# Six of the eleven down blocks of each FFN: half of each computed by seven products of 2x2 block sums

## What is computed

```python
def _swiglu(h, w_gu, w_down):
    g, u = jnp.split(h @ w_gu, 2, axis=-1)
    return (jax.nn.silu(g) * u) @ w_down

x = x + 0.5 * _rmsnorm(_swiglu(_rmsnorm(x, ffn1_pre_g), ffn1_w_gu, ffn1_w_down), ffn1_post_g)
...
x = x + 0.5 * _rmsnorm(_swiglu(_rmsnorm(x, ffn2_pre_g), ffn2_w_gu, ffn2_w_down), ffn2_post_g)
```

## Time and profile before

| | |
|---|---|
| median of 3 runs | 1080.36 us (1080.18 to 1080.76) |
| the profiled execution | 1081.31 us, span 1079.4 us |
| PE busy | 1068.7 us, 99% of the span |
| DVE busy | 789.1 us, 73% |
| ACT busy | 608.5 us, 56% |
| granted clock of PE | 1.00 of 2.4 GHz over the span |

### The profile page before, as it was taken

How to read it: one execution, slowest core, us unless ns; L and a number is a source line. 1 busy time by engine, 2 the same in 40 slices (tenths; PEclk the granted TensorE clock), 3 DMA queues, 4 the chain that set the end, 5 groups by cost and what they waited for, 6 DMA issues and landing times.

```text
span 1079.4 us, 21082 instructions
## 1 busy us (share of the span) xinstructions
PE 1068.7 (99%) x8534; PEld 1009.7 (94%) x8534; DVE 789.1 (73%) x1125; ACT 608.5 (56%) x905; POOL 0.2 (0%) x4
## 2 busy tenths in 40 slices
PE   9999999999999999999999999999999999999999
PEld 7999999999989999999999998999999799999898
DVE  5665556989979777778778555775655887997884
ACT  5544444678586545878445556444444575655471
POOL 0000000000000000000000000000000000000000
PEclk9999999999999999999999999999999999999999
DMA  9866556465543454444546533465556355542251
GB/s 343 292 213 211 176 182 209 151 221 174 179 154 121 152 181 157 157 164 149 208 166 244 196 106 130 147 230 198 188 182 212 119 177 200 191 157 95 102 196 39
DMA packets 29297, 190.71 MB, mean 177 GB/s; under 512 B 3656, under 2 KB 4521, under 8 KB 7466
## 3 DMA queue, kind: packets, MB, share of 16 engines
q1 hardware_dynamic: 26480, 182.53, 48.6%
q10 hardware_dynamic: 2746, 7.16, 1.9%
HBM read 188.62 MB, written 1.05 MB: 176 GB/s over the span
## 4 chain that ended last, share of the span: by engine, by line
PE 87%; DVE 9%; ACT 2%; issue 1%; DMA 1%; SPq 0%; DVEq 0%; ACTq 0%
PE bank L526 15%; PE bank L528 15%; PE bank L527 15%; PE bank L538 10%; PE bank L539 10%; PE bank L540 10%; DVE sb_w_lo L2098 3%; PE bank L625 2%; PE bank L761 1%; DVE sb_ssd_conv L2409 1%; DMA sb_w_raw<-in_w 1%; PE bank L709 1%; PE bank L886 1%; ACT sb_w_hi L1371 1%; PE bank L1048 1%
## 5 line engine op out<-in xcount | busy, mean ns | idle before, releaser
L2098 DVE TENSOR_TENSOR sb_w_lo<-sb_w_raw,sb_w_hi 128x2048 fp32r<-128x2048 f32 x169 | 386.4, 2289 | 118.9 <-ACT sb_w_hi L1371 118.5
L1371 ACT ACTIVATE sb_w_hi<-sb_w_raw 128x2048 fp32r<-128x2048 f32 x169 | 322.9, 1911 | 33.0 <-PE bank L528 29.2
L526 PE MATMUL bank<-sb_hT_hi,sb_w_hi 128*128 128x256 f32 (+1 forms) x816 | 225.7, 277 | 0.0
L528 PE MATMUL bank<-sb_hT_hi,sb_w_lo 128*128 128x256 f32 (+1 forms) x816 | 225.7, 277 | 0.0
L527 PE MATMUL bank<-sb_hT_lo,sb_w_hi 128*128 128x256 f32 (+1 forms) x816 | 225.6, 276 | 0.0
L538 PE MATMUL bank<-sb_hT_hi,sb_w_hi 128*128 128x256 f32 (+2 forms) x744 | 213.1, 286 | 0.2 <-DVE sb_hT_lo L2175 0.2
L539 PE MATMUL bank<-sb_hT_lo,sb_w_hi 128*128 128x256 f32 (+2 forms) x744 | 206.2, 277 | 0.0
L540 PE MATMUL bank<-sb_hT_hi,sb_w_lo 128*128 128x256 f32 x744 | 205.9, 277 | 0.0
L526 PEld LDWEIGHTS bank<-sb_hT_hi,sb_w_hi 128*128 128x128 f32 (+1 forms) x816 | 152.7, 187 | 0.0
L528 PEld LDWEIGHTS bank<-sb_hT_hi,sb_w_lo 128*128 128x128 f32 (+1 forms) x816 | 152.6, 187 | 0.0
L527 PEld LDWEIGHTS bank<-sb_hT_lo,sb_w_hi 128*128 128x128 f32 (+1 forms) x816 | 152.6, 187 | 0.0
(11 more groups left out here) (516 smaller groups left out, 2077.9 us busy)
## 6 DMA issues: line engine op xcount, KB each, us to landing
sb_w_raw<-in_w SPq DMA_DIRECT2D x169, 1024.0 KB, 4.9
sb_w_raw<-in_w SPq DMA_DIRECT2D x4, 512.0 KB, 7.8
sb_hT<-in_xT SPq DMA_DIRECT2D x2, 512.0 KB, 5.3
sb_x<-in_x SPq DMA_DIRECT2D x2, 512.0 KB, 11.8
sb_mem_xn<-in_mem ACTq DMA_DIRECT2D x1, 1024.0 KB, 7.1
sb_mem_T<-in_memT ACTq DMA_DIRECT2D x1, 1024.0 KB, 10.4
...
```

What stands on the lines that cost most here:

```text
L526: pe.matmul(o, a_hi, b_hi, start=first, stop=False)
L528: return pe.matmul(o, a_lo, b_hi, start=False, stop=last)
L1371: act.activation(w_hi[b % STAGES][:], w_raw[b % RING][:], ACT.Copy).then_inc(w_hi_in, 1)
L2098: tt(w_lo[b % STAGES][:], w_raw[b % RING][:], f32(w_hi[b % STAGES][:]), ALU.subtract).then_inc(w_lo_in, 1)
```

## The change

Per FFN the pairs 0, 1, 8, 9 and 10 stay plain. For the pairs 2 to 7 the half h = 0 of the down block, a product of a 2x2 grid of activation blocks (t, k) with a 2x2 grid of weight blocks (k, 256 columns), is computed by seven products of 128 x 128 x 256 in place of eight, from sums of blocks (a scheme of Strassen's kind, in Winograd's form); the half h = 1 stays as before, six passes of 512 columns for each token half. The seven products are summed over the six pairs in banks 3, 4, 5 and 6 and are joined once per FFN. A mixed block is thus 12 passes of 512 columns and 21 of 256, and its last product is not cut: the call passes no widths, so `parts` is (512,).

What this adds on the other engines: DVE forms three sums of the weights of a mixed block (`mix_block`, 512, 256 and 256 columns; one of them in place in `w_raw`), ACT rounds them (768 columns, with the block's own rounding, which now waits for the sums), DVE takes their low part (768 columns); of the activations of a pair DVE forms four sums of 128 columns, ACT rounds them, DVE takes the low part (512 columns). Per FFN: two products of zeros, 512 columns wide, in the middle of the up block 5, which open the banks 5 and 6; `join` (six DVE operations and two ACT copies) while pair 8 is in work; behind the FFN two more additions of 512 columns on DVE, the squares on ACT taken from the joined halves. The up blocks now alternate between two banks in place of three. The host puts the columns of the mixed blocks in another order (the half h = 1 first). The number and size of the weight transfers stay.

```diff
-PAIR_TURNS = PAIRS - 3
+PAIR_TURNS = PAIRS - 5
...
+SEVENS = range(2, PAIRS - 3)
+MIXED_PAIRS = len(SEVENS)
...
+                def up_bank(j):
+                    return 5 if n == 1 and j == 2 else (FIRST[f"ffn{n}"] + j % 2) % 3
...
-                    o = claim_turns([f"up{n}.{j + 2 * i}" for i in range(PAIR_TURNS)], b % 3, b, turn)
+                    o = claim_turns([f"up{n}.{j + 2 * i}" for i in range(PAIR_TURNS - 1)], up_bank(j), b, turn)
...
-                def down_block(c, turn=0, parts=(512,), all_three=False):
...
+                def last_product(o, w_hi, w_lo, parts, all_three):
+                    t = slice(P, SEQ)
+                    for m, (a, w) in enumerate(((f["hi"], w_hi), (f["hi"], w_lo), (f["lo"], w_hi))):
+                        at = 0
+                        for width in parts if all_three or m == 2 else (512,):
+                            mm = pe.matmul(o[:, at:at + width], a[:, 1, t], w[:, at:at + width], start=False, stop=False)
+                            at += width
+                    return mm
...
+                def mixed_block(c, turn=0, parts=(512,), all_three=False):
                     b = down_at(n, c)
                     pe.wait_ge(w_lo_in, b + 1 - SPLIT_FROM + TURN * turn)
+                    hi, lo = w_hi[b % STAGES], w_lo[b % STAGES]
+                    top, low = slice(0, P), slice(P, SEQ)
+                    b11, u2, b22, b21 = (slice(MIX_AT + i * 256, MIX_AT + (i + 1) * 256) for i in range(4))
+                    u1, u3, u4 = (slice(i * 256, (i + 1) * 256) for i in range(3))
+                    def plain_half(o, k, t):
+                        h = slice(PLAIN_AT + k * 512, PLAIN_AT + (k + 1) * 512)
+                        return product(o[:], f["hi"][:, k, t], f["lo"][:, k, t], hi[:, h], lo[:, h], False, False)
+                    def of_tile(bank, side, k, t, m_hi, m_lo, m, closes):
+                        product(banks[bank][:, side * 256:(side + 1) * 256], f["hi"][:, k, t], f["lo"][:, k, t],
+                                m_hi[:, m], m_lo[:, m], False, closes and c == SEVENS[-1])
+                    def of_sum(bank, side, i, m_hi, m_lo, m, closes):
+                        product(banks[bank][:, side * 256:(side + 1) * 256], sum_hi[:, i, :], sum_lo[:, i, :],
+                                m_hi[:, m], m_lo[:, m], False, closes and c == SEVENS[-1])
+                    tile_in(c, 0, turn)
+                    plain_half(banks[7], 0, top)
+                    tile_in(c, 1, turn)
+                    plain_half(banks[7], 1, top)
+                    of_tile(5, 0, 0, top, hi, lo, b11, False)
+                    of_tile(3, 0, 1, top, hi, lo, b21, False)
+                    of_tile(4, 0, 1, low, mix_hi, mix_lo, u4, True)
+                    pe.wait_ge(S("ffn_sum_lo"), MIXED_PAIRS * (n - 1) + c - SEVENS[0] + 1 + turn)
+                    of_sum(3, 1, 3, hi, lo, b22, True)
+                    of_sum(5, 1, 0, mix_hi, mix_lo, u1, True)
+                    of_sum(6, 0, 1, hi, lo, u2, False)
+                    of_sum(6, 1, 2, mix_hi, mix_lo, u3, True)
+                    plain_half(banks[last_bank], 0, low)
+                    last = slice(PLAIN_AT + 512, PLAIN_AT + 1024)
+                    last_product(banks[last_bank], hi[:, last], lo[:, last], parts, all_three).then_inc(block_done, 1)
...
+                def open_banks():
+                    pe.wait_ge(S("zero_r"), n)
+                    w = w_hi[up_at(n, 5) % STAGES]
+                    for q in range(2):
+                        open_mixed(n, q)
+                        pe.matmul(banks[5 + q][:], zero_r[:], w[:, 0:512], start=True, stop=False)
...
+                            if k and i == 3 and not last:
+                                mm = last_product(o, hi[:, 1, h], lo[:, 1, h], parts, all_three)
+                                continue
...
-                o = [claim(f"down{n}.{i}", 3 + i, down_at(n, PAIRS - 1) if i == 3 else None) for i in range(4)]
-                down_block(0, 0, *LAST_DOWN[n][0])
+                plain_block(0, *LAST_DOWN[n][0])
                 up_block(3)
-                with pe.Fori(0, PAIR_TURNS) as turn:
-                    up_block(4, turn)
-                    down_block(1, turn, *LAST_DOWN[n][1])
-                    up_block(5, turn)
+                up_block(4)
+                plain_block(1, *LAST_DOWN[n][1])
+                up_block(5, between=open_banks)
+                with pe.Fori(0, PAIR_TURNS - 1) as turn:
+                    up_block(6, turn)
+                    mixed_block(2, turn)
+                    up_block(7, turn)
+                for j in (FF_TILES - 6, FF_TILES - 4):
+                    up_block(j)
+                    c = j // 2 - 1
+                    if c in SEVENS:
+                        mixed_block(c)
+                    else:
+                        plain_block(c, *LAST_DOWN[n][1])
+                    up_block(j + 1)
...
-                down_block(PAIRS - 2, 0, *LAST_DOWN[n][2])
+                plain_block(PAIRS - 2, *LAST_DOWN[n][2])
...
-                down_block(PAIRS - 1)
+                plain_block(PAIRS - 1)
...
-                act.activation(w_hi[b % STAGES][:], w_raw[b % RING][:], ACT.Copy).then_inc(w_hi_in, 1)
+                if b in MIXED_OF:
+                    act.wait_ge(S("ffn_mixed"), MIXED_OF[b] + 1 + turn)
+                    act.activation(w_hi[b % STAGES][:], w_raw[b % RING][:], ACT.Copy)
+                    act.activation(mix_hi[:], mix_raw[:], ACT.Copy).then_inc(w_hi_in, 1)
+                else:
+                    act.activation(w_hi[b % STAGES][:], w_raw[b % RING][:], ACT.Copy).then_inc(w_hi_in, 1)
...
-                tt(w_lo[b % STAGES][:], w_raw[b % RING][:], f32(w_hi[b % STAGES][:]), ALU.subtract).then_inc(w_lo_in, 1)
+                ins = tt(w_lo[b % STAGES][:], w_raw[b % RING][:], f32(w_hi[b % STAGES][:]), ALU.subtract)
+                if b in MIXED_OF:
+                    ins = tt(mix_lo[:], mix_raw[:], f32(mix_hi[:]), ALU.subtract)
+                ins.then_inc(w_lo_in, 1)
+            def mix_block(b, turn=0):
+                w = w_raw[b % RING]
+                def quarter(first, last):
+                    return w[:, MIX_AT + first * 256:MIX_AT + last * 256]
+                dve.wait_ge(w_landed[b % RING], 16 * (b // RING + 1 + turn))
+                p = MIXED_OF[b]
+                tt(mix_raw[:, 0:512], quarter(0, 2), quarter(1, 3), ALU.add).then_inc(S("ffn_mixing"), 1)
+                dve.wait_ge(S("ffn_mixing"), 2 * p + 1 + 2 * turn)
+                tt(quarter(1, 2), mix_raw[:, 0:256], quarter(2, 3), ALU.add).then_inc(S("ffn_mixing"), 1)
+                dve.wait_ge(S("ffn_mixing"), 2 * p + 2 + 2 * turn)
+                tt(mix_raw[:, 512:768], quarter(1, 2), quarter(3, 4), ALU.add).then_inc(S("ffn_mixed"), 1)
...
+                def first_sum(c, turn):
+                    p = MIXED_PAIRS * (n - 1) + c - SEVENS[0]
+                    even = f["act"][:, 0, :]
+                    if p:
+                        dve.wait_ge(S("ffn_sum_hi"), p + turn)
+                    tt(sum_raw[:, 2, :], even[:, 0:P], even[:, P:SEQ], ALU.subtract).then_inc(S("ffn_summing"), 1)
+                def other_sums(c, turn):
+                    p = MIXED_PAIRS * (n - 1) + c - SEVENS[0]
+                    even, odd = f["act"][:, 0, :], f["act"][:, 1, :]
+                    dve.wait_ge(S("ffn_summing"), 2 * p + 1 + 2 * turn)
+                    tt(sum_raw[:, 1, :], sum_raw[:, 2, :], odd[:, P:SEQ], ALU.add)
+                    tt(sum_raw[:, 0, :], even[:, P:SEQ], odd[:, P:SEQ], ALU.subtract).then_inc(S("ffn_summing"), 1)
+                    dve.wait_ge(S("ffn_summing"), 2 * p + 2 + 2 * turn)
+                    tt(sum_raw[:, 3, :], odd[:, 0:P], sum_raw[:, 1, :], ALU.subtract).then_inc(S("ffn_sum"), 1)
+                def sums_low(c, turn):
+                    p = MIXED_PAIRS * (n - 1) + c - SEVENS[0]
+                    dve.wait_ge(S("ffn_sum_hi"), p + 1 + turn)
+                    tt(sum_lo[:], sum_raw[:], f32(sum_hi[:]), ALU.subtract).then_inc(S("ffn_sum_lo"), 1)
+                def join():
+                    wait_read(dve, f"mixed{n}.0")
+                    y, p5, w = f["joined"], f["parts"][:, 0, :], f["parts"][:, 1, :]
+                    o = full(dve, f"mixed{n}.1")
+                    link(tt(w, o[:, 0:256], y[:, 0, 0:256], ALU.subtract))
+                    link(tt(y[:, 0, 256:512], w, p5, ALU.add))
+                    tt(y[:, 1, 0:256], o[:, 256:512], w, ALU.subtract)
+                    read(tt(y[:, 1, 256:512], y[:, 0, 256:512], o[:, 256:512], ALU.subtract), f"mixed{n}.1")
+                    wait_read(dve, f"mixed{n}.1")
+                    for t in range(TOK):
+                        key = f"mixed{n}.{2 + t}"
+                        read(tt(y[:, t, :], full(dve, key)[:], y[:, t, :], ALU.add), key)
...
+                    mixed = j // 2 in SEVENS
+                    if mixed:
+                        wait_read(dve, f"up{n}.{j}", turn)
```

(24 more changed lines are left out.)

106 lines of the change are left out of this document (79 added, 27 removed).

## The result

The changed kernel takes 1084.24 us (median of six runs, 1083.66 to 1084.97) against 1080.56 for the kernel before, a ratio of 1.0035 (95% interval 1.0024 to 1.0045): slower by 3.7 us, 0.35%. The forecast was 1084.9 in a range of 1079.0 to 1086.3.

A forecast was written before the change was run, and what follows sets the result against it. PE, busy 99% of the span, was taken to bound the kernel. The terms 1.9 + 1.6 - 0.25 + 0.1 + 0.9 + 0.35 = +4.6 us on the median 1080.36 gave 1084.9 us, range 1079.0 to 1086.3.

The forecast's parts named there:

- The exit: Up blocks behind each mixed block: 96 passes at the long pace until the next down block, 0.42 us.
- the long pace: PE's passes of 256 columns starting 117.8 ns apart, 4.4 ns a pass over the short pace, and staying so.
- the products of zeros: Up blocks 5 and 6: two wide passes, an entry, then 72 passes at the long pace; +1.6 us for both FFNs.
- the block of the earlier trace: Block before the change whose first two passes are 258 wide: four passes in 0.48 us, then 32 at 113.4 ns.
- the short pace: PE's passes of 256 columns starting 113.4 ns apart in an undisturbed stream, half of 226.7 for 512 columns.
- A pair: Mixed block with its exit on PE: 5.65 us against 5.50 plain, 0.15 more; twelve pairs +1.9 us.
- the inner passes: The 21 passes of 256 columns inside a mixed block, at the long pace: 2.47 us, 0.09 of it for the pace.
- The first FFN's tail: Behind the first FFN: two more DVE additions, 1.2 us, some 0.3 hidden in the wait for ACT; +0.9 us.
- The second's: Tail behind the second FFN: of the same 0.9 us on DVE, +0.35 passed on to PE; bounds 0 and 0.9.
- The stall of the first turn: First FFN, PE's wait for the up block's weights, 0.26 us, goes since PE gets there later; -0.25 us.
- The bank of up block 2: Second FFN: up block 2 takes up block 0's bank, which DVE still reads when PE starts; +0.1 us.
- DVE: Mixed turn: DVE's chain with ACT's rounding estimated at 15.6 us against PE's 16.2 to 16.5; costed at nothing.

The follow-up runs named there:

- the widened passes: Changed kernel, first two passes of the up block behind a mixed block two columns wider: 1084.33 us; eight columns wider: 1083.97 us in one run.
- the sevens last, tiles first: Changed kernel with the seven products moved to the mixed block's end, three with a tile stationary before four with a sum: 1083.95 us, ratio 1.0033.
- the uncut kernel: Kernel before the change, with the cut in its looped down blocks taken out: 1086.27 us, ratio 1.0054.
- the sevens last with tiles last: Changed kernel with the seven products at the mixed block's end, four of sums ahead of three of tiles: 1080.44 us in one run.
- the run with one more operation: Changed kernel with mixed blocks' last product cut, plus one unused 1024-column DVE operation in every mixed pair: 1089.53 us, ratio 1.0075.

## Why the prediction was right, and where it was not

**The exit** carried the forecast, and its outcome held: 96 passes at 117.8 ns behind each mixed block, in the place and at the price named. The cut takes it away (4.5 to 4.7 us), and taking the cut out of the kernel before brings it there (5.7 us in sixteen pairs, 0.36 each).

**Its generalisation was wrong in three places.** "Every change from 512 columns to 256 without a cut or a widened pass leads to the long pace" fails behind the products of zeros, which end uncut and lead to the short one; so that term was 0.48 an FFN and not 0.79, 1.0 in all for 1.6. It fails for the widened passes, which do not help here, and of which the block of the earlier trace rows itself came right in the kernel before and not in the changed one. And no change of width is needed: the sevens last, tiles first, hand the long pace on from narrow passes.

**What fits instead** is read from the last pass ahead of the boundary, between passes with moving weights and a block with moving activations. Four such passes, of the zeros, of a mixed block, and (in the kernel before, then in the changed one) of what stands ahead of the block of the earlier trace rows:

```profile
51.74 0.40 PE L828 MATMUL bank<-sb_w_hi,sb_zero_r 128*128 128x512 f32 x1
...
81.61 0.39 PE L776 MATMUL bank<-sb_w_hi,sb_ffn_lo 128*128 128x512 f32 x1
```

```profile
917.69 0.40 PE L528 MATMUL bank<-sb_w_hi,sb_ckv_lo 128*128 128x512 f32 x1
```

```profile
920.09 0.39 PE L543 MATMUL bank<-sb_w_hi,sb_ckv_lo 128*128 128x512 f32 x1
```

The first and the third last 0.40 us and reach 236 ns to the next start: the short pace follows. The second and the fourth last 0.39 and reach 227: the long pace follows. So it is at every boundary into a block with `hT` or the memory moving, in the thirteen traces (before, after and the eleven runs), whose last pass has 512 or 256 columns and which has no wait in it or in the 24 passes behind. Where the last pass took its shortest time to the next start (225 to 227 ns for 512 columns, 113 or 114 for 256), the block ran at the long pace, 80 times of 80; where it took longer (231 and more, 116 and more), at the short pace, 169 of 169. That covers the uncut kernel (227), the cut (116 to 121), the sevens last with tiles last (120) or sums last (113), the zeros and both outcomes of the earlier trace rows. It is a rule read from the traces, not a cause: the time of the last pass ends with the first start of the block, so the rows do not say which sets the other. It says nothing of waits, of last passes narrower than 256 columns, nor of the passes of the earlier trace rows, where weights move on both sides.

By it the forecast had some luck in its exit. The six uneven passes that end a mixed block take 232, 236, 229, 232, 231 and 227 ns; the sixth is one of the shortest, and that, rather than the change of width or the missing cut, is what goes with the long pace. The two passes of zeros end on a 236, and there the same argument failed.

**A pair** cost 5.61 us with its exit, forecast 5.65: the inner passes 2.43 for 2.47, since only nine of 21 were long, and the entries less. 12 x 0.10 = 1.2 in place of 1.9.

**The other terms.** The first FFN's tail 1.0 for 0.9, of which 0.8 is the longer wait at `kv2` and 0.2 the long pace that it happened to leave. The second's 0.21 for 0.35. The stall of the first turn went, as said: 6 x 0.10 + 0.48 - 0.26 = 0.82 is what the first FFN shows, 0.85. The bank of up block 2 was mis-sized, 0.46 for 0.1: the wait was counted and not the long pace that it left on the whole block here.

**DVE** was cheap only because its chain just fits: about 15.7 us, by estimate from the run with one more operation, against a turn of 16.49, or 16.11 with the cut.

The terms on record come to 4.6, those measured to 1.2 + 1.0 - 0.26 + 0.46 + 1.0 + 0.21 = 3.6, and the runs to 3.7. The two largest terms, the pairs and the zeros, were both put too high, by 0.7 and 0.6; that the sum lies within 1 us is owed in small part to the bank, put too low by 0.36.
